# The last expert's rows added on chip for two token tiles, which are read ahead of the last scatter

## What is computed

```
aff = softmax(h @ w_router);  vals, idx = top_k(aff.T, 128)        # 16 experts choose 128 tokens each
hid = silu(h[idx] @ w_gate) * (h[idx] @ w_up)
y   = (hid @ w_down) * vals
x   = x + ga2 * zeros.at[idx].add(y)                               # each expert's 128 rows are added
x   = rmsnorm(x, g_final)                                          # end of the first block
z   = rms_norm(x, even_ln_g) @ even_w_in                           # "aq", "ak", "av", ... by columns
```

## Time and profile before

| | |
|---|---|
| median of 3 runs | 2996.09 us (2995.45 to 2996.61) |
| the profiled execution | 2995.05 us, its span 2993.2 us |
| PE busy | 2766.7 us, 92% of the span |
| DVE, ACT, POOL busy | 1692.2, 1403.2, 211.0 us |
| chain that ended last | PE 82%, DVE 9%, ACT 4%, issue 2%, DMA 2% |

### The profile page before, as it was taken

How to read it: one execution, slowest core, us unless ns; L and a number is a source line. 1 busy time by engine, 2 the same in 40 slices (tenths; PEclk the granted TensorE clock), 3 DMA queues, 4 the chain that set the end, 5 groups by cost and what they waited for, 6 DMA issues and landing times.

```text
span 2993.2 us, 38224 instructions
## 1 busy us (share of the span) xinstructions
PE 2766.7 (92%) x13888; PEld 2062.8 (69%) x13902; DVE 1692.2 (57%) x3157; ACT 1403.2 (47%) x2557; POOL 211.0 (7%) x248
## 2 busy tenths in 40 slices
PE   7999999999993899999989988999999989989998
PEld 3567794888772677777757755775677766866676
DVE  1368373334467788888846468545534556536523
ACT  2333272223242666666636356535622547437411
POOL 0000000000010010000015000000020000000500
PEclk9999999999996999999999999999999999999999
DMA  9510110322434899999965100301132201000321
GB/s 371 200 57 29 63 51 1 141 85 87 155 145 165 305 378 377 377 377 378 377 201 161 21 22 8 85 1 53 34 113 72 83 15 58 29 18 19 113 85 56
DMA packets 178458, 401.60 MB, mean 134 GB/s; under 512 B 7948, under 2 KB 9004, under 8 KB 177792
## 3 DMA queue, kind: packets, MB, share of 16 engines
q1 hardware_dynamic: 158224, 329.27, 31.0%
q0 software_dynamic: 19936, 70.26, 7.2%
q10 hardware_dynamic: 144, 0.01, 0.0%
HBM read 363.70 MB, written 35.81 MB: 133 GB/s over the span
## 4 chain that ended last, share of the span: by engine, by line
PE 82%; DVE 9%; ACT 4%; issue 2%; DMA 2%; SPq 0%; DVEq 0%; POOL 0%; POOLq 0%; ACTq 0%
PE psum L303 8%; PE psum L788 7%; PE psum L790 7%; PE psum L789 7%; PE psum L1486 5%; PE psum L1488 5%; PE psum L1487 5%; PE psum L1621 4%; PE psum L1431 3%; PE psum L1430 3%; PE psum L1429 3%; PE psum L1639 3%; PE psum L1663 3%; PE psum L1724 2%; PE psum L1726 2%
## 5 line engine op out<-in xcount | busy, mean ns | idle before, releaser
L789 PE MATMUL psum<-ring_r,kctx_r 128*128 128x512 f32 (+1 forms) x544 | 214.1, 394 | 0.0
L789 PE MATMUL psum<-ring_r,cols_r 128*128 128x512 f32 (+1 forms) x544 | 212.9, 391 | 0.0
L2133 ACT ACTIVATE ring<-ring,att 128x256 f32<-128x256 f32 (+7 forms) x256 | 173.1, 676 | 48.7 <-DVE att L2778 48.7
L2632 DVE TENSOR_TENSOR ring_r<-ring,pair_r 128x1024 fp32r<-128x1024 f32 x128 | 148.1, 1219 | 51.6 <-ACT pair_r L2011 51.6
L1621 PE MATMUL psum<-wide 64*128 64x512 f32 (+2 forms) x704 | 149.2, 504 | 17.4 <-DVE att L2778 14.4
L1487 PE MATMUL psum<-ring_r,wide_r 128*128 128x512 f32 x384 | 151.3, 394 | 0.0
L627 DVE TENSOR_TENSOR ring_r<-ring,ring_r 128x1024 fp32r<-128x1024 f32 x48 | 58.7, 1225 | 129.7 <-ACT ring_r L624 129.3
L1429 PE MATMUL psum<-small_r,ring_r 128*128 128x512 f32 x320 | 125.8, 393 | 0.8 <-DVE pair L2502 0.8
L1431 PE MATMUL psum<-small_r,ring_r 128*128 128x512 f32 x320 | 126.3, 395 | 0.0
L2011 ACT ACTIVATE pair_r<-ring 128x1024 fp32r<-128x1024 f32 x128 | 124.4, 1046 | 0.0
L1639 PE MATMUL psum<-ident,ring 128*128 128x128 f32 x640 | 116.6, 290 | 6.4 <-DVE ring L2805 6.3
(11 more groups left out here) (558 smaller groups left out, 7174.1 us busy)
## 6 DMA issues: line engine op xcount, KB each, us to landing
ring<-in_w_gate SPq DMA_DIRECT2D x64, 1024.0 KB, 9.6
ring<-in_w_up SPq DMA_DIRECT2D x32, 1024.0 KB, 9.8
hidden<-in_w_up SPq DMA_DIRECT2D x32, 1024.0 KB, 9.8
hidden<-in_w_down SPq DMA_DIRECT2D x32, 1024.0 KB, 8.6
pair<-in_w_down SPq DMA_DIRECT2D x32, 1024.0 KB, 8.7
ring<-in_w_ada SPq DMA_DIRECT2D x24, 1024.0 KB, 14.7
ring<-in_w_in SPq DMA_DIRECT2D x24, 1024.0 KB, 7.2
ring<-in_even_w_in SPq DMA_DIRECT2D x16, 1024.0 KB, 13.3
```

The costliest lines, as they stand in the source:

```text
L789: self.eng.matmul(outp, XHIGH[b][:, k, :], low[:, k, 0:wd], start=False, stop=False)
```

## The change

- Tiles 0 and 1 are read from `acc` by one DMA on ScalarE's queue as soon as 15 of the 16 scatters have landed. The last scatter waits for that read (`x2_in3`), since it would change the rows that are read.
- The last expert's rows for these tiles are added on chip. A matrix `onehot` (128 slots x 256 tokens) has a one where the slot's token is that token; VectorE makes it by comparing a row of token numbers (a new input, broadcast by one more GpSimd DMA early on) with the expert's indices. ScalarE rounds each half of `yb`, VectorE subtracts, TensorE multiplies by `onehot` (8 products of 128x512), VectorE adds the four results to `x1` (`x2_add`).
- SyncE's reads become tiles 2 to 3 and tiles 4 to 7, both right after the last scatter.
- `s2.weights()` is broken up: piece 0 goes between the two squares of tile 0, piece 1 behind its second root, piece 2 behind its evacuation, piece 3 behind `s2.rows`. ScalarE also waits for the last scatter before `s2.rows`, whose output overwrites the indices.
- GpSimd waits for the last scatter before `gained(1)` instead of before `gained(0)`.
- TensorE no longer waits for x before its 16 fillers.

```diff
-        X2_PARTS = ((0, 1), (1, 4), (4, 8))
+        X2_PARTS = ((0, 2), (2, 4), (4, 8))
+        ADDED = 2
...
         def x2_ready(eng, t):
+            if t < ADDED:
+                eng.wait_ge(S("x2_add"), before("x2_add") + t + 1)
+                return
...
                     for i, (t0, t1) in enumerate(X2_PARTS):
+                        if t1 == ADDED:
+                            continue
                         sp.dma_start(x1[:, t0:t1, :], scratch["acc"].rearrange("(t p) n -> p t n", p=P)[:, t0:t1, :]).then_inc(S(f"x2_in{3 + i}"), 16)
-                        if i == 0:
-                            x2_ready(sp, 0)
...
+            pool.dma_start(token_row, a["token_row"].partition_broadcast(P)).then_inc(S("gf"), 16)
...
+                if early:
+                    pool.wait_ge(S("x2_in3"), before("x2_in3") + 16)
                 pool.indirect_dma_start(scratch["acc"], bass.IndirectOffsetOnAxis(idx1[:, 1:2].bitcast(U32), 0), yb, None,
                                         compute_op=ALU.add).then_inc(S("moe_sct"), 16)
-                pool.wait_ge(S("moe_sct"), e * 16)
+                if not early:
+                    pool.wait_ge(S("moe_sct"), e * 16)
...
                     x2_ready(pool, t)
+                    if t == 1:
+                        pool.wait_ge(S("moe_sct"), 16 * NEXP)
...
             down(NEXP)
+            for m in range(2):
+                ms = slice(m * HALF, (m + 1) * HALF)
+                pe.wait_ge(S("last_low"), before("last_low") + m + 1)
+                for t in range(ADDED):
+                    pe.matmul(last_bank(m, t), onehot[:, span(t)], XSH[:, ms], start=True, stop=False)
+                    pe.matmul(last_bank(m, t), onehot[:, span(t)], XSL[:, ms], start=False, stop=True).then_inc(S("last_mm"), 1)
...
-            x2_ready(pe, 0)
             filler(16)
...
-            act.wait_ge(S("moe_y"), 2 * NEXP)
-            s2.weights()
+            act.wait_ge(S("moe_u"), 2 * NEXP)
+            act.wait_ge(S("moe_sct"), 16 * (NEXP - 1))
+            act.dma_start(x1[:, 0:ADDED, :], scratch["acc"].rearrange("(t p) n -> p t n", p=P)[:, 0:ADDED, :]).then_inc(S("x2_in3"), 16)
+            for m in range(2):
+                ms = slice(m * HALF, (m + 1) * HALF)
+                act.wait_ge(S("moe_y"), 2 * NEXP - 1 + m)
+                act.activation(XSH[:, ms], yb[:, ms], ACT.Copy).then_inc(S("last_high"), 1)
             act.activation(stat[:, 62:63], epsc[:, 0:1], ACT.Sqrt)
-            stats(0)
+            stats(0, lambda: s2.piece(0))
             root(0)
+            s2.piece(1)
             N3.evac_act(act, 0)
             N3.done(act, 0)
+            s2.piece(2)
+            act.wait_ge(S("moe_sct"), 16 * NEXP)
             s2.rows(H2[0][:, :, span(0)])
+            s2.piece(3)
             stats(1)
...
+            link(dve.tensor_copy(last_slot, idxc[:, NEXP - 1:NEXP]))
+            dve.wait_ge(S("gf"), 32)
+            link(dve.tensor_scalar(onehot, token_row, last_slot, None, ALU.is_equal))
             dve.wait_ge(S("moe_sct"), 16 * NEXP - 16)
-            output(NEXP - 1, 0)
-            output(NEXP - 1, 1)
+            for m in range(2):
+                ms = slice(m * HALF, (m + 1) * HALF)
+                output(NEXP - 1, m)
+                dve.wait_ge(S("last_high"), before("last_high") + m + 1)
+                dve.tensor_tensor(XSL[:, ms], yb[:, ms], XSH[:, ms].bitcast(F32), ALU.subtract).then_inc(S("last_low"), 1)
+            dve.wait_ge(S("x2_in3"), before("x2_in3") + 16)
+            for t in range(ADDED):
+                for m in range(2):
+                    ms = slice(m * HALF, (m + 1) * HALF)
+                    dve.wait_ge(S("last_mm"), before("last_mm") + (ADDED * m + t + 1))
+                    ins = dve.tensor_tensor(x1[:, t, ms], x1[:, t, ms], last_bank(m, t), ALU.add)
+                ins.then_inc(S("x2_add"), 1)
...
-            s2.weights()
+            s2.piece(0)
             sums(0)
             norms(0)
+            s2.piece(1)
             N3.evac_dve(dve, 0)
             N3.done(dve, 0)
+            s2.piece(2)
             s2.rows(H2[0][:, :, span(0)])
+            s2.piece(3)
```

More of the change, by code:

```diff
@@ L147, in build @@
         share("gpsimd", [("mirror", {"ed": 4}), ("gain", {"ed": TT}), ("r0norm", {"ed": 4}), ("r1norm", {"ed": 16})])
-        share("ready", [("r_high", {"": 1}), ("hm_mm", {"": TT}), ("part_sum", {"": TT}), ("moe_hhigh", {"": NEXP - 1})])
-        share("taken", [("r_low", {"": 1}), ("hm_ev", {"": TT}), ("part_out", {"": TT}), ("moe_hlow", {"": NEXP - 1})])
-        share("few", [("sel", {"_mm": 1})] + [(p, {"_mm": 1}) for p in ("gate", "mid", "dn", "forget")])
+        share("ready", [("r_high", {"": 1}), ("hm_mm", {"": TT}), ("part_sum", {"": TT}), ("moe_hhigh", {"": NEXP - 1}), ("last_high", {"": 2})])
+        share("taken", [("r_low", {"": 1}), ("hm_ev", {"": TT}), ("part_out", {"": TT}), ("moe_hlow", {"": NEXP - 1}), ("last_low", {"": 2}), ("x2_add", {"": 2})])
+        share("few", [("sel", {"_mm": 1})] + [(p, {"_mm": 1}) for p in ("gate", "mid", "dn")] + [("last", {"_mm": 4}), ("forget", {"_mm": 1})])
         share("dram", [(p, {"_out": 16, "_in": 16}) for p in ("hT", "fu")])
@@ L572, in build, with last_bank @@
         MSPLIT = 5
+        token_row, onehot = extra[:, 0:ADDED * P], split["extra"][:, HALF:HALF + ADDED * P]
+        last_slot = firsts[:, 0:1]
+        def last_bank(m, t):
+            return bank((6, 7, 4, 5)[2 * m + t])
         HDH, HDL = split["sel_wT"][:, 0:D], split["small"][:, 2 * D:3 * D]
@@ L990, in _, with one @@
             pool.indirect_dma_start(xg, None, scratch["xn"], bass.IndirectOffsetOnAxis(idx1[:, 0:1].bitcast(U32), 0)).then_inc(S("moe_gat"), 16)
-            def one(e, more):
+            def one(e, more, early=False):
                 if more:
@@ L1008, in _ @@
             one(NEXP - 1, False)
-            one(NEXP, False)
-            pool.wait_ge(S("gf"), 16)
+            one(NEXP, False, early=True)
+            pool.wait_ge(S("gf"), 32)
             for t in range(TT + 1):
@@ L2230, in last_norms_act, with stats @@
                     N4.done(act, TT - 1)
-            def stats(t):
+            def stats(t, aside=None):
                 x2_ready(act, t)
@@ L2239, in stats @@
                 act.activation(stat[:, 16 + t:17 + t], stat[:, t:t + 1], ACT.Sqrt, bias=epsc[:, 0:1], scale=1.0 / D).then_inc(S("nf_rt"), 1)
+                if aside:
+                    aside()
                 act.wait_ge(S("gained"), before("gained") + t + 1)
@@ L3049, in host_layout @@
         "strip_a": strip_a, "strip_c": strip_c, "strip_d": strip_d,
+        "token_row": np.arange(2 * P, dtype=np.float32),
         "b_gate": bg, "sel": sel.reshape(64 + NG, -1),
```

## The result

In 20 executions of each on one chip the changed kernel took 3000.43 us (2998.21 to 3006.0) and the kernel before 2996.74 us (2992.35 to 3002.49): ratio 1.0014, 95% interval 1.0008 to 1.0021. That is just inside the 0.2% that counts as no change, as forecast, but 2.9 us above the forecast time and 1.4 us above the range. The profiled execution took 2998.85 us with a span of 2997.0 us, against 2995.05 and 2993.2.

A forecast was written before the change was run, and what follows sets the result against it. TensorE is busy 92% of the span, but a chain of waits from the last expert's output sets tile 1's transposes. Seven terms, -2.7 -0.9 +0 +3.0 +0.9 +2.0 -0.85, gave +1.4 us on 2996.09: 2997.5 us, range 2991.5 to 2999.0.

The forecast's parts named there:

- Premise: Whole kernel: the change is worth only what it moves the start of tile 1's transposes at 1583.70; later row tiles keep their rhythm.
- base: Time of the kernel before, to which the forecast change was added: the median of 2996.09 us.
- Term 4: Tile 0's norms: VectorE's 128x1 product meets the whole of GpSimd's gained(1), and xn is slowed beside xb; +3.0 us.
- Term 6: ScalarE between tile 0's evacuation and tile 1's first square: pieces 2 and 3 now stand there at 1.0 us each; +2.0 us.
- Term 1: Tile 0's data: read landed at 1563.8, additions done by 1565.15 instead of 1567.87; -2.7 us.
- The 33 packets from the gathers: DMA queue: 33 packets per engine stand ahead of a newcomer, so the read waits 6.4 us behind "aq".
- rival B: The read takes turns with "aq" at once, and piece 0 may become the bound; middle -2.3 us, chance 0.25.
- Terms 2 and 3: Tile 0: fillers no longer hold its transposes, -0.9 us; piece 0 just fits between its squares, 0.
- A2: Scatter lands 0.3 us later, xn already runs and GpSimd waits, so the gained(1) meeting costs nothing; -1.6 us, chance 0.23.
- Term 7: Tile 1's norms: VectorE's 128x1 product meets no gained, while xn still meets xb; -0.85 us.
- Term 5: Tile 1's transposes: TensorE, idle for over 5 us, runs them at half clock; +0.9 us.
- C: An engine leaving its loop fetches code behind the queued packets, after the read's landing; +7.8 us, 3003.9 us, chance 0.05.

The follow-up runs named there:

- e3_fillers: The changed kernel with 38 instead of 10 TensorE fillers between the transposes of tiles 0 and 1; 2998.12 us, 1.0008 of the kernel before.
- d: The changed kernel with GpSimd's gained of tiles 1 and 2 multiplying by constant 1 instead of g_final, so one input; 2995.87 us, 1.0001 of the kernel before.
- g3: The kernel before, unchanged, run once more for its trace; 2996.89 us, ratio 1.0004.
- h3: The kernel before with 26 instead of 16 fillers ahead of tile 0's transposes, meant as a pure delay; 2998.37 us, ratio 1.0010.
- a_again: The changed kernel, unchanged, run once more; 3002.73 us, 1.0021 of the kernel before.
- b_read_first: The changed kernel with the read of tiles 0 and 1 on SyncE's queue ahead of the first attention weights; 3000.16 us, 1.0011 of the kernel before.
- f3: The changed kernel with the read first on SyncE's queue, gained[1] elsewhere, pieces behind both tiles' norms, 22 fillers for 10; 2992.25 us, 0.9989 of the kernel before.
- k: The reordered version f3, unchanged, run once more; 2994.67 us, 0.9994 of the kernel before.
- i: The reordered version f3 with row tile 0's split ahead of the four pieces and 13 fillers instead of 22; 2996.74 us, 0.9997 of the kernel before.

## Why the prediction was wrong, by its steps

- **Premise: only the start moves, then a fixed rhythm.** This is the step that failed, and with the base it holds all of the 2.9 us. Start of tile 1's transposes: +1.2 measured, +1.4 forecast. Behind it, where nothing was counted, +0.9 in the first product, by the half clock (e3_fillers against after shows that the clock is what costs there), and +1.65 in the attention layer in the profiled execution (with the clock, by the table above; that this part belongs to the change isn't shown). Inside the stretch two more steps failed, terms 4 and 6, and cancelled. The base was 0.65 us low: before's median is 2996.09 in 3 executions and 2996.74 in 20.
- **Term 1** (-2.7): right, 12.6 us for the read and -2.8 at tile 0's first square. The 33 packets from the gathers gave the wait nearly: 1.3 + 6.4 = 7.7 us to the first packet by the forecast, and in after's trace none moves in the 7 us behind the issue at 1551.80 but one, just ahead of 1559. The rule of the Trainium skill, "DMA: Bandwidth & Descriptors", section "Queues, rings and completion order", that each engine goes round robin between queues, was rival B; by the trace the read got no turn in those 7 us, and half of the engines' time from 1559 to 1562 us.
- **Terms 2 and 3** (-0.9, 0): right. Only 0.35 us of the 0.9 shows between the first square and tile 0's transposes, because `gained` of tile 0 took 0.5 us longer beside the additions, which the forecast left out. Piece 0 fits before the second square.
- **Term 4** (+3.0): not there. The first L2984 took 0.16 us, the sign that was named for A2, and `gained` of tile 1 started at 1571.25, 0.2 us behind xn: rival A2's miss. But the prediction stopped there, as if a miss were free.
- **Term 6** (+2.0): mis-sized by the sentence that "VectorE's halves of them run beside". They don't run beside GpSimd. Missed by xn, `gained` stopped the next subtraction for 2.15 us, and the one of tile 2 stopped another (felt in term 7). Between tile 0's transposes and tile 1's first square it is 7.21 us instead of 3.24: 4.0 more, where terms 5 and 6 had 2.9; the other 1.1 come from the first of these collisions.
- **Term 5** (+0.9): the transposes ran at half clock as forecast (1.97 instead of 1.04 us), but the collision held VectorE's evacuation longer, so the 0.9 can't be read by itself. And the clock was booked at one place where it falls due at two: tile 1's transposes ran at half clock before as well, but of the product behind them 9 multiplications do instead of 5.
- **Term 7** (-0.85): L2984 of tile 1 took 0.66 instead of 1.01, and xn 0.75 instead of 1.58, so 1.2 us are saved there, where 0.85 were forecast: this xn runs wholly inside xb (1583.54 to 1586.38) and isn't slower, against the "xn still meets xb" of the forecast. The 1.90 us wait for L2977 takes them back.
- **Rivals.** A2 happened as a mechanism and did not give its -1.6. B and C didn't happen. That the forecast start was right to 0.2 us was luck: term 4 was 3.0 us too much, and the others together 2.7 too little.

What stays open is the attention layer. Its length goes with the granted clock in every trace, but why the clock falls more often in the changed kernels (of the ten traces with the new code only d's is as good as before's and g3's) isn't settled. h3, with the old code and a shift, falls too, and after and a_again, the same kernel, differ by 3.4 us of missing clock. It may be the moment at which the layer begins, or chance in single executions. Ahead of 1540 us, where the code hardly differs, the traces differ as well: 47.8 us of clock are missing in before, 49.5 in after and 52.9 in a_again and d. More traces of one kernel would tell.

## What to carry to other kernels

When data is to be ready sooner, list what the sooner work of GpSimd will run beside. The two-input GpSimd operation stopped a VectorE operation in nearly every meeting here, so a meeting avoided at one instruction is paid at the next, unless the whole order is made for it. Count a start that moves together with the clock that TensorE has there, up to the end of the next product. And where a kernel's executions spread by 10 us, one trace of each is no ledger for 4: compare the stretch in the traces and the means of many executions.

## What the runs showed of the hardware

- A transfer of 1 MB on an idle queue, beside a queue that is being drained, took 12.6 to 12.7 us in six kernels; ahead of it, on the same queue, 6.2 us in b_read_first and 4.9 to 5.3 in f3, k and i. The scatter behind it then took 11.4 to 11.9 us instead of 6.4.
- Two-input `gained` against VectorE: subtractions of two tensors took 2.93 to 3.39 us instead of 1.2, a one-input xn 2.92 instead of 0.75 (a_again), a 128x1 product 2.14 instead of 0.16 (f3). The Trainium skill, "SBUF — State Buffer", section "SBUF: two separate sides", has this as a lock that the loser waits out, and these rows agree. Against the one-input GpSimd operation of d the subtraction took 1.88 and ended inside it, which the section's rule for two-input VectorE operations doesn't give. In after xn started 0.21 us ahead of `gained` and ran on, while `gained` took 2.75 instead of 2.34; in a_again it is shown 0.03 us ahead and was stopped, but GpSimd's times are too rough to say who was first there.
- TensorE's granted clock in the attention layer differed between executions of one kernel: 8.5 us of it were missing in after and 12.0 in a_again, and the layer took 1.65 and 4.4 us longer than before.
